# Neighbourhood attention: context and latent head pairs alternate, and GpSimd scales each pair's second head

## The chip, the cores and the metric

The kernel runs on one core of a Trainium2 chip. The metric is the device time of one execution, in microseconds (us). Before the change the median of three runs is 2026.64 us (2026.27 to 2027.99).

## What is computed

A two-layer backbone over 256 latent and 256 context tokens. The even layer's mixer has eight neighbourhood-attention heads of width 64 beside four mLSTM heads. The change touches the attention heads alone. Cut to what matters:

```python
def context_attention(q, k, v):                      # 256 context queries, 256 context keys
    s = jnp.einsum('bqhd,bkhd->bhqk', q, k) * (q.shape[-1] ** -0.5)
    p = jax.nn.softmax(s, axis=-1)
    return jnp.einsum('bhqk,bkhd->bqhd', p, v)

def neighbourhood_attention(q, k, v, k_ctx, v_ctx, rpb):   # 256 latent queries
    # one softmax over a clamped 4 x 16 window of the latent grid (with a learned bias)
    # and all 256 context keys
    logits = concatenate([s_loc + bias, s_ctx], -1)
    p = softmax(logits)
    return p_loc @ vwin + p_ctx @ v_ctx
```

The kernel computes the latent rows against all 512 tokens, context first, and a bias of -1e30 takes out the latent keys that are outside the window.

## The kernel before, in words

Each engine has its own program, written out by hand; semaphores tie them together. Attention is done in 32 units: a head pair `hp` (0 to 3), a stream `st` (0 context with 256 keys, 1 latent with 512 keys), a tile `qt` of 128 queries (0 or 1) and one of the pair's two heads `hh`. Two units that differ only in `hh` form a pair `p` of the loops (0 to 15). In this document "first head" and "second head" are these two, and a "round" is the four pairs of one `hp`.

What happens to pair `p`:

- TensorE `scores(p)` (L880) writes both heads' scores into two of four score banks.
- VectorE `maxima(p)` finds the negated row maximum. For a context unit that is one reduction from the bank (L2192). For a latent unit it is a copy of the context columns (L2194), an addition of the bias (L2195) and a reduction over 512 columns (L2196).
- ScalarE `exps(p)` (L1464) takes the exponential into `probs` and sums the rows.
- VectorE takes the reciprocal of the sums (L2204) and multiplies each head's probabilities by it (L2207).
- TensorE transposes them in 128x128 blocks (L909): 2 blocks for a context unit, 4 for a latent one.
- ScalarE `turned_probs(p)` (L1475) copies them to `probsT`.
- When both query tiles of a stream are there, TensorE `weigh` (L892) multiplies them with the values. VectorE `attention_out` (L2291) copies the result out.

The order in which VectorE works is `maxima(p + 1)`, then reciprocal and multiplications of pair `p`. TensorE does `scores(p + 2)`, then the transposes of `p`, then perhaps a `weigh`. `maxima(p)` waits until the transposes of `p - 2` are done (semaphore `na_pT_done`), as it reuses their `probs` buffers.

Before the change the order within a head pair is context, context, latent, latent. In the program listings below, `L` and `R` are regions of SBUF in which `probs` lies, and `bank` is one of the eight PSUM banks.

Of the kernel before, what the change touches and what calls it, by code (L numbers as in the profile page):

```python
# [20 lines left out]
ALU = mybir.AluOpType  # L21
# [6 lines left out]
CTX, LAT = 256, 256  # L28
T = CTX + LAT
# [72 lines left out]
def build(nc, i, out, stop=None):  # L102

    stack = contextlib.ExitStack()
    with stack:
        def sb(name, shape):
            return stack.enter_context(nc.sbuf_tensor(name, shape, F32))
# [3 lines left out]
        def sem(name):  # L111
            if name not in sems:
                sems[name] = stack.enter_context(nc.semaphore(name))
            return sems[name]
# [87 lines left out]
        col = sb("col", [P, 12])  # L202
# [64 lines left out]
        probs = [L[:, 0:T], L[:, T:2 * T], R[:, 12288:12288 + T], R[:, 5120:5120 + T]]  # L267
# [99 lines left out]
        ret_s = view(R, 9216, 4, TT, LAT)  # L367


        UNITS = [(hp, st, hh, qt) for hp in range(4) for st in range(2) for qt in range(2) for hh in range(2)]  # L370
        NA_PAIRS = len(UNITS) // 2


# [175 lines left out]
        def _(pe):  # L549
# [270 lines left out]
            def even():  # L820
# [46 lines left out]
                def scores(p):  # L867
# [7 lines left out]
                    for u in (2 * p, 2 * p + 1):  # L875
                        hp, st, hh, qt = UNITS[u]
                        r0 = NA_DIM * hh
# [5 lines left out]
                def weigh(group):  # L883

                    hp, st = group // 2, group % 2
                    tiles = 2 if st == 0 else 4
                    pe.wait_ge(sem("na_pT_ready"), 4 * group + 4)
                    if group >= 2:
                        pe.wait_ge(sem("even_y0"), group - 1)
                    for kt in range(tiles):  # L890
                        for hh in range(2):
                            last = nc.tensor.matmul(banks[4 + group % 2][NA_DIM * hh:NA_DIM * (hh + 1), 0:CTX],  # L892
                                                    na_v[:, kt, (2 * hp + hh) * NA_DIM:(2 * hp + hh + 1) * NA_DIM],
                                                    probsT(st, hh)[:, kt, :], start=(kt == 0), stop=(kt == tiles - 1))
                            if kt == tiles - 1:
                                last.then_inc(sem("na_out_done"), 1)
# [3 lines left out]
                for p in range(NA_PAIRS):  # L900
                    if p + 2 < NA_PAIRS:
                        scores(p + 2)
                    for u in (2 * p, 2 * p + 1):
                        tiles = 2 if UNITS[u][1] == 0 else 4
                        pe.wait_ge(sem("na_probs_ready"), u + 1)
                        if p:
                            pe.wait_ge(sem("na_pT_ready"), u - 1)
                        for kt in range(tiles):
                            last = nc.tensor.transpose(banks[2 + u % 2][:, kt * P:(kt + 1) * P], probs[u % 4][:, kt * P:(kt + 1) * P], ident[:, :])  # L909
                        last.then_inc(sem("na_pT_done"), 1)  # L910
                    if p and p % 2 == 0:
                        weigh(p // 2 - 1)
                weigh(NA_PAIRS // 2 - 1)


# [195 lines left out]
        def _(act):  # L1111
# [291 lines left out]
            def even():  # L1403
# [53 lines left out]
                def exps(p):  # L1457

                    for u in (2 * p, 2 * p + 1):
                        st = UNITS[u][1]  # L1460
                        keys = CTX if st == 0 else T
# [5 lines left out]
                def turned_probs(p):  # L1467

                    for u in (2 * p, 2 * p + 1):
                        hp, st, hh, qt = UNITS[u]  # L1470
                        tiles = 2 if st == 0 else 4
                        act.wait_ge(sem("na_pT_done"), u + 1)
                        if p >= 4 and qt == 0:
                            act.wait_ge(sem("na_out_done"), 2 * (p // 2) - 2)
                        nc.scalar.activation(probsT(st, hh)[:, :, qt * P:(qt + 1) * P],  # L1475
                                             banks[2 + hh][:, 0:tiles * P].rearrange("p (a n) -> p a n", n=P), ACT.Copy).then_inc(sem("na_pT_ready"), 1)

# [128 lines left out]
        def _(dve):  # L1606
# [4 lines left out]
            def link(ins):  # L1611

                chain[0] += 1
                ins.then_inc(sem("dve_chain"), 1)
                dve.wait_ge(sem("dve_chain"), chain[0])
# [509 lines left out]
            def even():  # L2125
# [7 lines left out]
                for hd in range(HEADS):  # L2133
# [5 lines left out]
                    for j in (0, 1, 3, 4):  # L2139
                        sh = j - CONV // 2  # L2140
                        a, b = max(0, -sh), CTX - max(0, sh)
# [57 lines left out]
                for p in range(NA_PAIRS):  # L2199
                    if p + 1 < NA_PAIRS:  # L2200
                        maxima(p + 1)
                    a = 2 * (p % 2)
                    dve.wait_ge(sem("na_exp_done"), 2 * p + 2)
                    link(nc.vector.reciprocal(col[:, 8 + a:10 + a], col[:, 4 + a:6 + a]))  # L2204
                    for u in (2 * p, 2 * p + 1):
                        keys = CTX if UNITS[u][1] == 0 else T
                        nc.vector.tensor_scalar(probs[u % 4][:, 0:keys], probs[u % 4][:, 0:keys], col[:, 8 + u % 4:9 + u % 4], None,  # L2207
                                                ALU.mult).then_inc(sem("na_probs_ready"), 1)
                    if p >= 3 and p % 2:
                        attention_out(p // 2 - 1)  # L2210
                attention_out(NA_PAIRS // 2 - 1)


                dve.wait_ge(sem("even_acol_ready"), 2)
# [71 lines left out]
            def attention_out(group):  # L2286

                hp, st = group // 2, group % 2
                a, b = STREAMS[st]
                dve.wait_ge(sem("na_out_done"), 2 * group + 2)  # L2290
                nc.vector.tensor_copy(y[:, hp, a:b], banks[4 + group % 2][:, 0:CTX]).then_inc(sem("even_y0"), 1)  # L2291
# [102 lines left out]
        def _(pool):  # L2394
            def sums(name, c0):

                w = slice(c0, T)
                for d in range(KT - 1):
                    if name == "ffn2":
                        cosines(d)  # L2400
                    pool.wait_ge(sem("r_ready"), before("r_ready", name) + d + 1)
                    if d == 0:
                        nc.gpsimd.tensor_copy(rsum[:, w], h[:, 0, w]).then_inc(sem("sums"), 1)  # L2403
                    else:
                        nc.gpsimd.tensor_tensor(rsum[:, w], rsum[:, w], h[:, d, w], ALU.add).then_inc(sem("sums"), 1)  # L2405
                    at = stages.index(name)
                    pool.wait_ge(sem("sq"), (KT - 1) * at + halves(name, streams(name)[0]) + d + 1)
                    if d == 0:
                        nc.gpsimd.tensor_copy(rsq[:, w], sq[:, 0, w]).then_inc(sem("sums"), 1)
                    else:  # L2410
                        nc.gpsimd.tensor_tensor(rsq[:, w], rsq[:, w], sq[:, d % 2, w], ALU.add).then_inc(sem("sums"), 1)
                    pool.wait_ge(sem("sums"), before("sums", name) + 2 * d + 2)
                if name == "ffn2":
                    cosines(KT - 1)
# [24 lines left out]
            def causal(buf, way, fill=0.0):  # L2439

                sign = 1 if way == 0 else -1
                return nc.gpsimd.affine_select(out=buf, in_=buf, pattern=[[sign, P]], compare_op=ALU.is_ge, fill=fill,
                                               base=0, channel_multiplier=-sign)

            def even():

                nc.gpsimd.memset(L[:, 0:2560], 0.0)
                nc.gpsimd.memset(R[:, 4096:6144], 0.0).then_inc(sem("s5_zero"), 1)
                pool.wait_ge(sem("even_conv_done"), HEADS)
                nc.gpsimd.memset(R[:, 12288:13312], 0.0).then_inc(sem("s5_zero"), 1)  # L2450
                for k in range(1, len(BATCHES) // 2):
                    pool.wait_ge(sem("s5_local_written"), 16 * k)
                    nc.gpsimd.memset(R[:, 12288:12800], 0.0).then_inc(sem("s5_zero"), 1)
                pool.wait_ge(sem("s5_local_written"), 16 * (len(BATCHES) // 2))
                for b in range(2):
                    pool.wait_ge(sem(f"s5_ops_written{b}"), 32 * (len(BATCHES) // 2))
                nc.gpsimd.memset(ml_v[:, :, :, HDIM:VCOLS], 1.0).then_inc(sem("ml_ready"), 1)
                nc.gpsimd.memset(outside, 0.0).then_inc(sem("s5_zero"), 1)
                pool.wait_ge(sem("s5_zero"), 2 + len(BATCHES) // 2)
                for way in range(2):  # L2460
                    causal(outside[:, way, :], way, -1e30).then_inc(sem("ml_ready"), 1)
                sums("even", 0)
                centre("even")
                gains(1, "even", 0)
# [192 lines left out]
```

## Time and profile before

| | us |
|---|---|
| median of three runs | 2026.64 |
| the profiled execution | 2024.13 |
| its span | 2022.4 |
| TensorE busy in the span | 1917.7 |
| VectorE busy | 1263.6 |
| ScalarE busy | 644.7 |
| GpSimd busy | 290.5 |

The attention stage lies between 629.7 us (first scores) and 699.0 us (last output copied) of the span. A page of the profile gives shares over the whole span; what a change in this stage is worth has to be read from the stage itself, for which the views take a window.

### The profile page before, as it was taken

To read this page: it belongs to the slowest core of one execution; us is meant where nothing else is said; L and a number is where in the kernel's file an instruction comes from. 1 tells how busy PE (TensorE), PEld (TensorE's weight loads), DVE (VectorE), ACT (ScalarE), POOL (GpSimd) and SP (SyncE) were. 2 spreads that over 40 slices of the span, in tenths; PEclk is the share of its full clock that TensorE was granted. 3 is DMA by queue.
4 is the path that set the end of the run, shared out by engine and by line. 5 is a ranking of instruction groups with operands and counts; after the bars stand their busy time and mean duration, and the time that the engine had idled before them with its cause. 6 is when DMAs were issued, how large, how long until landed. Compare 5 with 4: busy or idle time off the path is not lost.

```text
span 2022.4 us, 24268 instructions
## 1 busy us (share of the span) xinstructions
PE 1917.7 (95%) x9246; PEld 1523.2 (75%) x9246; DVE 1263.6 (62%) x2215; ACT 644.7 (32%) x1093; POOL 290.5 (14%) x318
## 2 busy tenths in 40 slices
PE   5999999999998789899999989999999899989997
PEld 5888878885553454788887878888778867879997
DVE  7677776742883572777778357774777535464454
ACT  2322242323343431422224233222423232334442
POOL 0000001150000002400000231000044535130003
PEclk7999999998998899899999999999999999989999
DMA  9354535313360001355444233544134544214542
GB/s 361 126 204 170 206 142 162 135 54 125 115 231 9 1 1 42 121 201 198 177 161 183 95 150 121 203 179 155 73 117 190 222 180 177 84 42 167 186 164 108
DMA packets 43959, 290.12 MB, mean 143 GB/s; under 512 B 13916, under 2 KB 19676, under 8 KB 27232
## 3 DMA queue, kind: packets, MB, share of 16 engines
q1 hardware_dynamic: 34336, 270.08, 35.6%
q10 hardware_dynamic: 9536, 18.88, 2.5%
q8 instruction: 55, 0.90, 0.2%
q14 instruction: 32, 0.26, 0.0%
HBM read 272.16 MB, written 16.78 MB: 143 GB/s over the span
## 4 chain that ended last, share of the span: by engine, by line
PE 84%; DVE 9%; ACT 3%; DMA 2%; issue 1%; POOL 1%; SPq 0%; ACTq 0%; POOLq 0%; DVEq 0%
PE bank L613 13%; PE bank L618 13%; PE bank L615 13%; PE bank L670 7%; PE bank L679 6%; PE bank L676 6%; PE bank L807 4%; PE bank L804 3%; PE bank L791 3%; PE bank L1001 2%; PE bank L744 2%; PE bank L734 1%; PE bank L998 1%; DVE L L1729 1%; PE bank L956 1%
## 5 line engine op out<-in xcount | busy, mean ns | idle before, releaser
L1729 DVE CUSTOM_DVE_ANT_0 L<-slot 128x1024 f32<-128x1024 f32 x272 | 337.7, 1241 | 72.1 <-DMA slot<-in_ada_dram 64.9
L1185 ACT ACTIVATE w_hi<-slot 128x1024 fp32r<-128x1024 f32 x176 | 186.2, 1060 | 571.4 <-PE bank L618 559.2
L1786 DVE TENSOR_TENSOR w_lo<-slot,w_hi 128x1024 fp32r<-128x1024 f32 x176 | 216.9, 1235 | 217.8 <-ACT w_hi L1185 212.0
L613 PE MATMUL bank<-m_hi,w_hi 128*128 128x512 f32 (+1 forms) x1344 | 296.6, 363 | 3.2 <-ACT w_hi L1185 3.2
L615 PE MATMUL bank<-m_lo,w_hi 128*128 128x512 f32 (+1 forms) x1344 | 296.1, 362 | 0.0
L618 PE MATMUL bank<-m_hi,w_lo 128*128 128x512 f32 (+1 forms) x1344 | 296.1, 362 | 0.0
L613 PEld LDWEIGHTS bank<-m_hi,w_hi 128*128 128x128 f32 x1344 | 232.3, 189 | 43.1 <-ACT w_hi L1185 4.0
L615 PEld LDWEIGHTS bank<-m_lo,w_hi 128*128 128x128 f32 x1344 | 232.6, 189 | 39.3
L618 PEld LDWEIGHTS bank<-m_hi,w_lo 128*128 128x128 f32 x1344 | 232.6, 189 | 39.3
L1945 DVE TENSOR_TENSOR down_lo<-slot,down_hi 128x1408 fp32r<-128x1408 f32 x64 | 108.6, 1709 | 128.5 <-ACT down_hi L1235 128.3
L676 PE MATMUL bank<-g_lo,down_hi 128*128 128x512 f32 (+1 forms) x770 | 156.5, 351 | 0.1
L676 PEld LDWEIGHTS bank<-g_lo,down_hi 128*128 128x128 f32 x770 | 128.1, 193 | 19.6 <-DVE g_lo L1951 0.8
L1235 ACT ACTIVATE down_hi<-slot 128x1408 fp32r<-128x1408 f32 x64 | 87.6, 1377 | 158.0 <-PE bank L679 119.7
L2403 POOL COPY L<-h 128x512 f32<-128x512 f32 (+1 forms) x6 | 3.6, 607 | 910.1 <-DVE h L1826 910.1
L670 PE MATMUL bank<-g_hi_mid,down_hi 128*128 128x512 f32 (+1 forms) x420 | 99.6, 367 | 1.8 <-ACT g_hi_mid L1245 1.5
L679 PE MATMUL bank<-g_hi_mid,down_lo 128*128 128x512 f32 (+1 forms) x420 | 88.7, 347 | 0.0
L670 PEld LDWEIGHTS bank<-g_hi_mid,down_hi 128*128 128x128 f32 x420 | 72.3, 195 | 20.2 <-ACT g_hi_mid L1245 9.9
L807 PE MATMUL bank<-m,slot 128*128 128x512 f32 x192 | 85.5, 602 | 0.0
L679 PEld LDWEIGHTS bank<-g_hi_mid,down_lo 128*128 128x128 f32 x420 | 69.5, 189 | 9.9
L2405 POOL TENSOR_TENSOR L<-L,h 128x512 f32<-128x512 f32 (+1 forms) x36 | 43.7, 1213 | 219.9 <-DVE h L1826 219.4
L807 PEld LDWEIGHTS bank<-m,slot 128*128 128x128 f32 x192 | 36.7, 194 | 43.9 <-issue 43.9
L2424 POOL TENSOR_TENSOR h<-h,L 128x256 f32<-128x256 f32 x80 | 63.4, 829 | 36.4 <-DVE L L1855 36.4
(348 smaller groups left out, 2616.8 us busy)
## 6 DMA issues: line engine op xcount, KB each, us to landing
slot<-in_gateup_dram SPq DMA_DIRECT2D x44, 2048.0 KB, 7.5
slot<-in_ada_dram SPq DMA_DIRECT2D x34, 2048.0 KB, 7.5
slot<-in_down_dram SPq DMA_DIRECT2D x32, 1408.0 KB, 5.9
slot<-in_ev_in_dram SPq DMA_DIRECT2D x4, 2048.0 KB, 9.7
slot<-in_od_in_dram SPq DMA_DIRECT2D x4, 2048.0 KB, 10.1
R<-s_ops SPq DMA_DIRECT2D x16, 512.0 KB, 6.8
s_tables<-slot ACTq DMA_DIRECT2D x8, 768.0 KB, 3.3
R<-s_tables SPq DMA_DIRECT2D x8, 768.0 KB, 7.4
```

Source lines behind the costliest of these rows:

```text
L613: nc.tensor.matmul(bank[j][:, c0:T], w_hi[:, off, c, :], m_hi[:, c, c0:T], start=(c == 0), stop=False)
L615: nc.tensor.matmul(bank[j][:, c0:T], w_hi[:, off, c, :], m_lo[:, c, c0:T], start=False, stop=False)
L618: last = nc.tensor.matmul(bank[j][:, c0:T], w_lo[b][:, 2 * j + off, c, :], m_hi[:, c, c0:T], start=False, stop=(c == KT - 1))
L670: nc.tensor.matmul(out_d, down_hi[:, half, f % HALF, :], g_hi(f)[:, a:b], start=(f == 0), stop=False)
L676: nc.tensor.matmul(out_d, down_hi[:, half, f % HALF, :], g_lo[:, f, a:b], start=False, stop=False)
L679: last = nc.tensor.matmul(out_d, down_lo[k - 3][:, half, f % HALF, :], g_hi(f)[:, a:b], start=False, stop=(f == FT - 1))
L807: last = nc.tensor.matmul(banks[n % 4][:, c0:T], wslot(k)[:, j, c, :], m[:, c, c0:T], start=(c == 0), stop=(c == KT - 1))
L1185: nc.scalar.activation(w_hi[:, off, :, :].rearrange("p a b -> p (a b)"), slots[b][:, (2 * (f % 2) + off) * D:(2 * (f % 2) + off + 1) * D], ...
L1235: nc.scalar.activation(down_hi[:, half, :, :].rearrange("p a b -> p (a b)"), slots[k][:, half * HALF * P:(half + 1) * HALF * P], ACT.Copy) ...
L1729: ins = nc.vector.tensor_tensor_reduce(out=junk, in0=slots[k][:, t * D:(t + 1) * D], in1=csilu[s_], scale=1.0, scalar=0.0, op0=ALU.mult, o ...
L1786: nc.vector.tensor_tensor(w_lo[b][:, t, :, :].rearrange("p a b -> p (a b)"), slots[b][:, t * D:(t + 1) * D], w_hi[:, off, :, :].bitcast(F3 ...
L1945: nc.vector.tensor_tensor(down_lo[d % 2][:, half, :, :].rearrange("p a b -> p (a b)"), slots[3 + d % 2][:, half * HALF * P:(half + 1) * HA ...
```

## The change

The order of the units becomes context, latent, context, latent within a head pair. The `weigh` of a stream moves to where its second query tile has been transposed: the context one behind the fourth pair of its head pair, the latent one behind the first pair of the next. `attention_out` moves accordingly, and so does the wait in `turned_probs`. The multiplication of each pair's second head moves from VectorE to GpSimd, which now waits for the reciprocals through a new semaphore `na_rec_ready`. TensorE waits for the first head on `na_probs_even` and for the second on `na_probs_odd`.

```diff
-        UNITS = [(hp, st, hh, qt) for hp in range(4) for st in range(2) for qt in range(2) for hh in range(2)]
+        UNITS = [(hp, st, hh, qt) for hp in range(4) for qt in range(2) for st in range(2) for hh in range(2)]
...
-                    pe.wait_ge(sem("na_pT_ready"), 4 * group + 4)
+                    pe.wait_ge(sem("na_pT_ready"), 2 * (4 * hp + 3 + st))
...
-                        pe.wait_ge(sem("na_probs_ready"), u + 1)
+                        pe.wait_ge(sem("na_probs_odd") if u % 2 else sem("na_probs_even"), p + 1)
...
-                    if p and p % 2 == 0:
-                        weigh(p // 2 - 1)
+                    if p % 4 == 3:
+                        weigh(p // 4 * 2)
+                    if p % 4 == 0 and p:
+                        weigh(p // 4 * 2 - 1)
...
-                            act.wait_ge(sem("na_out_done"), 2 * (p // 2) - 2)
+                            act.wait_ge(sem("na_out_done"), 2 * (2 * (hp - 1) + st) + 2)
...
-                    link(nc.vector.reciprocal(col[:, 8 + a:10 + a], col[:, 4 + a:6 + a]))
-                    for u in (2 * p, 2 * p + 1):
-                        keys = CTX if UNITS[u][1] == 0 else T
-                        nc.vector.tensor_scalar(probs[u % 4][:, 0:keys], probs[u % 4][:, 0:keys], col[:, 8 + u % 4:9 + u % 4], None,
-                                                ALU.mult).then_inc(sem("na_probs_ready"), 1)
-                    if p >= 3 and p % 2:
-                        attention_out(p // 2 - 1)
-                attention_out(NA_PAIRS // 2 - 1)
+                    nc.vector.reciprocal(col[:, 8 + a:10 + a], col[:, 4 + a:6 + a]).then_inc(sem("na_rec_ready"), 1)
+                    dve.wait_ge(sem("na_rec_ready"), p + 1)
+                    keys = CTX if UNITS[2 * p][1] == 0 else T
+                    nc.vector.tensor_scalar(probs[a][:, 0:keys], probs[a][:, 0:keys], col[:, 8 + a:9 + a], None, ALU.mult).then_inc(sem("na_probs_even"), 1)
+                    if p >= 4 and p % 4 < 2:
+                        attention_out(2 * (p // 4) - 2 + p % 4)
+                for group in range(NA_PAIRS // 2 - 2, NA_PAIRS // 2):
+                    attention_out(group)
...
+                for p in range(NA_PAIRS):
+                    u = 2 * p + 1
+                    keys = CTX if UNITS[u][1] == 0 else T
+                    pool.wait_ge(sem("na_rec_ready"), p + 1)
+                    nc.gpsimd.tensor_scalar(probs[u % 4][:, 0:keys], probs[u % 4][:, 0:keys], col[:, 8 + u % 4:9 + u % 4], None,
+                                            ALU.mult).then_inc(sem("na_probs_odd"), 1)
```

On TensorE (L880 scores, L909 transposes, L892 `weigh`, of which a latent one is eight rows and a context one the row with x4), before, from the transposes of a round's first latent pair on:

```order
L909 MATMUL bank<-ident,L 128x128 x8
L892 MATMUL bank<-L,R 64x256 x4
L880 MATMUL bank<-R 128x256 x2
L909 MATMUL bank<-ident,R 128x128 x8
L880 MATMUL bank<-R 128x512 x2
L909 MATMUL bank<-ident,L 128x128 x4
L892 MATMUL bank<-L,R 64x256
L892 MATMUL bank<-R 64x256
```

The same engine now, from the transposes of a round's last latent pair to those of the next round's first latent pair:

```order
L909 MATMUL bank<-ident,R 128x128 x8
L892 MATMUL bank<-L,R 64x256 x4
L880 MATMUL bank<-R 128x256 x2
L909 MATMUL bank<-ident,L 128x128 x4
L892 MATMUL bank<-L,R 64x256
L892 MATMUL bank<-R 64x256
...
L880 MATMUL bank<-R 128x512 x2
L909 MATMUL bank<-ident,R 128x128 x8
```

The context `weigh` has moved from in front of a latent pair's transposes to in front of a context pair's. The latent `weigh` has moved from behind a context pair with another context pair to follow, to behind a context pair with a latent pair's scores and transposes to follow.

On VectorE, before, from the reciprocal of a round's second context pair on (L2194 to L2196 are the maxima of a latent unit):

```order
L2204 RECIPROCAL col<-col 128x2 [waits na_exp_done]
L2207 TENSOR_SCALAR R<-R,col 128x256 [waits dve_chain]
L2207 TENSOR_SCALAR R<-R,col 128x256
L2291 COPY m<-bank5 128x256 [waits na_out_done]
L2194 COPY R<-bank7 128x256 [waits na_scores_done,na_pT_done]
```

VectorE now, at the same place of a round, with the line numbers of the changed file (the reciprocal is L2206, the multiplication L2209, the context reduction L2194):

```order
L2206 RECIPROCAL col<-col 128x2 [waits na_exp_done]
L2209 TENSOR_SCALAR L<-L,col 128x256 [waits na_rec_ready]
L2293 COPY m<-bank4 128x256 [waits na_out_done]
L2194 TENSOR_REDUCE col<-bank0 128x1 [waits na_scores_done,na_pT_done]
L2194 TENSOR_REDUCE col<-bank1 128x1 [waits na_scores_done]
L2206 RECIPROCAL col<-col 128x2 [waits na_exp_done]
L2209 TENSOR_SCALAR R<-R,col 128x512 [waits na_rec_ready]
```

One multiplication stands behind each reciprocal where there were two, and context reductions stand between the work of two latent pairs.

## Rows read from the trace of the kernel before

**Rows 1.** Windows: the attention stage (busy us per engine, TensorE clock share, DMA)
```profile
628.00:700.00 72.00, 53.50 (x274) 29.30 (x274) 44.62 (x120) 35.99 (x99) 0.00 (x0) 0.76 0.00 1
```
**Rows 2.** Timeline of VectorE: start, duration, instruction [idle before, releaser]
```profile
630.51 1.42 DVE L2192 TENSOR_REDUCE col<-bank 128x1 f32<-128x256 f32 x4 [24.46 <-PE bank L880]
...
649.22 0.76 DVE L2192 TENSOR_REDUCE col<-bank 128x1 f32<-128x256 f32 x2 [1.61 <-PE bank L909]
649.90 0.15 DVE L2204 RECIPROCAL col<-col 128x2 f32<-128x2 f32 x1
...
651.23 0.42 DVE L2194 COPY L<-bank 128x256 f32<-128x256 f32 x1 [0.53 <-PE bank L909]
...
655.35 0.42 DVE L2194 COPY R<-bank 128x256 f32<-128x256 f32 x1 [0.20 <-PE bank L909]
...
658.12 0.15 DVE L2204 RECIPROCAL col<-col 128x2 f32<-128x2 f32 x1
...
660.86 0.76 DVE L2192 TENSOR_REDUCE col<-bank 128x1 f32<-128x256 f32 x2 [1.67 <-PE bank L909]
661.53 0.15 DVE L2204 RECIPROCAL col<-col 128x2 f32<-128x2 f32 x1
...
665.50 0.76 DVE L2192 TENSOR_REDUCE col<-bank 128x1 f32<-128x256 f32 x2 [2.27 <-PE bank L909]
...
680.56 0.76 DVE L2192 TENSOR_REDUCE col<-bank 128x1 f32<-128x256 f32 x2 [1.19 <-PE bank L909]
...
698.61 0.42 DVE L2291 COPY m<-bank 128x256 f32<-128x256 f32 x1 [4.05 <-PE bank L892]
```
**Rows 3.** Windows of the stage, columns as in rows 1 (clock is third from last)
```profile
634.00:643.00 9.00, 5.44 (x18) 2.44 (x16) 6.65 (x17) 4.36 (x11) 0.00 (x0) 0.50 0.00 1
...
648.00:658.00 10.00, 7.21 (x46) 3.62 (x44) 7.84 (x21) 5.76 (x16) 0.00 (x0) 1.00 0.01 2
658.00:665.00 7.00, 6.15 (x26) 4.04 (x27) 3.29 (x10) 2.96 (x9) 0.00 (x0) 0.51 0.00 0
...
689.00:695.00 6.00, 4.81 (x21) 3.35 (x22) 2.87 (x8) 2.01 (x5) 0.00 (x0) 0.50 0.00 0
```
**Rows 4.** Timeline of TensorE in the stage
```profile
635.09 2.08 PE L880 MATMUL bank<-R 64*128 64x512 f32 x4
...
648.09 1.09 PE L909 MATMUL bank<-ident,R 128*128 128x128 f32 x8
649.12 1.13 PE L880 MATMUL bank<-R 64*128 64x512 f32 x4
...
651.12 0.43 PE L892 MATMUL bank<-L,R 128*64 128x256 f32 x1
...
652.69 0.38 PE L892 MATMUL bank<-R 128*64 128x256 f32 x1
...
654.61 0.70 PE L909 MATMUL bank<-ident,R 128*128 128x128 f32 x4 [0.48 <-DVE R L2207]
...
658.85 1.97 PE L909 MATMUL bank<-ident,L 128*128 128x128 f32 x8 [2.91 <-DVE L L2207]
660.75 1.98 PE L892 MATMUL bank<-L,R 128*64 128x256 f32 x8
```
**Rows 5.** Groups by line and form, 628 to 700 us: VectorE's multiplication
```profile
L2207 DVE TENSOR_SCALAR L<-L,col 128x512 f32<-128x512 f32 x8 | 3.5, 484 | 0.1
L2207 DVE TENSOR_SCALAR L<-L,col 128x256 f32<-128x256 f32 x8 | 2.5, 351 | 0.1
```
**Rows 6.** GpSimd's tensor-scalar at L2436 (x: min/median/max ns), two windows
```profile
L2436 POOL TENSOR_SCALAR h<-h,lng,lnb x2: 772/773/774, 841.0 to 841.7; 128x512 f32<-128x512 f32 x2
...
L2436 POOL TENSOR_SCALAR h<-h,lng,lnb x8: 554/560/1229, 2014.7 to 2019.5; 128x256 f32<-128x256 f32 x8
```
**Rows 7.** VectorE's tensor-scalar at L1861 over the whole span
```profile
L1861 DVE TENSOR_SCALAR L<-L x10: 293/294/815, 411.6 to 2009.2; 128x256 f32<-128x256 f32 x10
```
**Rows 8.** Timeline at 1585 us: GpSimd and VectorE together
```profile
1584.64 2.87 POOL L2424 TENSOR_TENSOR h<-h,L 128x256 f32<-128x256 f32 x4
...
1585.39 0.81 DVE L1861 TENSOR_SCALAR L<-L 128x256 f32<-128x256 f32 x1
```

## Prediction, made before the changed kernel ran

> **What bounds the stage now.** I read the windows first, then VectorE's timeline, then TensorE's. The windows show that nothing is full in the 72 us of the attention stage: TensorE 53.5 us busy, VectorE 44.6, ScalarE 36.0, GpSimd none [rows 1]. So the stage is a chain that passes from engine to engine, and the timeline shows which. VectorE computes the maxima of a pair. Then it takes reciprocal and multiplications of the pair before, and then it sits idle until TensorE has transposed exactly those: all idle times before L2192 and L2194 from 649 us on end on L909 [rows 2]. I call the time from a pair's reciprocal to VectorE's next maxima the pair's turn. It holds the reciprocal, the multiplication, TensorE's queue and the transposes. Freeing VectorE from work that lies beside the transposes gives nothing; the turn counts.
>
> A round (four pairs) is then four maxima and four turns. Maxima take 655.35 to 658.12 = 2.77 us for a latent pair and 660.86 to 661.53 = 0.67 for a context pair [rows 2], so 6.88 a round in either order. Turns before: context 649.90 to 651.23 = 1.33; first latent 658.12 to 660.86 = 2.74; second latent 661.53 to 665.50 = 3.97 [rows 2]. 6.88 + 2 x 1.33 + 2.74 + 3.97 = 16.25, and the round from 649.22 to 665.50 is 16.28. The next, to 680.56, is 15.06. The first took 18.7 (630.51 to 649.22), the last with its end 18.5 (680.56 to 698.61 + 0.42). Together 68.5 us.
>
> The second number behind these is TensorE's clock: it is granted at 0.50 (1.2 GHz) in 634 to 643, at 1.00 (2.4 GHz) in 648 to 658, 0.51 in 658 to 665, and 0.50 in 689 to 695 [rows 3]. The fall at 658 comes while TensorE idles for 2.91 us during a latent pair's maxima [rows 4]; the rise comes after several us of unbroken work. Eight transposes take 1.97 us at the low level and 1.09 at the high; a latent pair's scores 2.08 and 1.13; a context `weigh` (8 rows of the trace) 1.98 at the low one [rows 4]. The latent `weigh` runs from 651.12 to 652.69 + 0.38 = 1.95 at the high one [rows 4]; twice that, 3.9, is my estimate for the low one, and half of 1.98, 1.0, for a context one at the high.
>
> **The multiplication on GpSimd.** VectorE takes 484 ns for 512 columns and 351 for 256 [rows 5]. GpSimd's nearest operation, L2436, which multiplies and adds, takes 772 ns and 554 with nothing in its way [rows 6]. Its slow cases reach 1229 [rows 6]. The trace of before has no single multiplication on GpSimd, so I bound it below by VectorE's own 484 and 351 and above by 1229, and take 772 and 554, the same form with one operation more.
>
> When does it start? Both engines are released by the same reciprocal, and both want SBUF. L1861 on VectorE, the same kind of operation, takes 293 ns at its fastest and 815 at its slowest [rows 7], and the slow one of 0.81 us lies inside GpSimd's L2424 [rows 8]: it was held 0.52 us. So the two don't run together. VectorE needs no hand-over between engines, so I take it as first; GpSimd starts when it ends. The Trainium skill, "SBUF — State Buffer", section "Who interferes with whom", says that a VectorE operation in a two-port mode and a GpSimd one exclude each other for a whole instruction and that the one issued first wins; by that rule the time comes out as in this sum or as in the third rival below, and the trace's 0.81 us agrees that one is held.
>
> Context turn, at the high clock: reciprocal to multiplication 0.19, first head 0.35, hand-over 0.06 (658.85 less the end of a 484 ns multiplication begun 0.19 after 658.12 [rows 2, 4, 5]), second head 0.55, hand-over 0.06, its two transposes 0.43 (four take 0.70, 0.27 of it for two), 0.05 to VectorE: 1.69 against 1.33, so 0.36 lost. What covered the second multiplication before was the first head's transposes; a GpSimd multiplication is longer than that cover. Second latent turn: 0.19 + 0.48 + 0.06 + 0.77 + 0.06 + 0.60 (four transposes, a little over half of 1.09) + 0.05 = 2.21 at the high clock. At the low one TensorE's scores of the pair after next, 2.08 us from the context turn's end, make the transposes wait: 2.08 + 1.97 - 0.67 + 0.1 = 3.5.
>
> **The moved order.** First latent turn: TensorE is now behind. After the context transposes stand the latent `weigh`, then a latent pair's scores, then the transposes; VectorE's part beside them is 0.67 of maxima. High: 1.95 + 1.10 + 1.04 - 0.67 - 0.1 = 3.3 (start to start, as 648.09 to 649.12; the 0.1 is the hand-over at either end). Low: 3.9 + 2.08 + 1.97 - 0.77 = 7.2. Before, this `weigh` ran beside a latent pair's maxima (651.12, inside 651.23 to 654), where 2.77 us hid it. What lies there now is the context `weigh`, 1.0 to 2.0 us, which before stood in the second latent turn and made it 3.97 instead of 2.74. VectorE's output copies stay beside TensorE's work, and ScalarE, 36 us busy of 72, has the exponentials done before each reciprocal as before; I cost both at nothing. If that cover went, each copy would cost 0.42. No DMA and no queue of SyncE is in the moved part; GpSimd has nothing else to do until the layer's norm.
>
> A round at the high clock: 6.88 + 2 x 1.69 + 3.3 + 2.2 = 15.8. With the second half low (context turn 2.0, second latent 3.5, after 2.8 us of idle TensorE as at 658): 17.4. Before: 15.06 and 16.28, mean 15.67. With the last round, for three rounds: from +0.4 to +5; I take +2.5. The first round starts the same way; at the low clock its sum is equal to before within 0.5 us, and as TensorE works more evenly there it may come back to the high clock earlier, worth up to 2.5: I take -1. The end: before 3.2 us from the last transposes to the last copy; now a context `weigh` and a latent one follow, 1.0 + 1.95 + 0.5 = 3.4 high, up to 6.4 low: I take +1. Sum +2.5 us. That is 2026.6 on the profiled execution's 2024.13; on the median of the runs, which is 2.5 above that execution, 2029.1.
>
> A measurement of this kernel can tell about 0.2%, 4 us, from no change.
>
> **Rivals.**
>
> 1. Faster. GpSimd's multiplication runs beside VectorE's without being held: context turns 1.33, latent 1.9 (0.36 x 8 and 0.3 x 4 less), and the evener TensorE work keeps the clock high in most of the stage. Rounds of 14.8 against 15.67, a first round of 16 against 18.7: -2.8 - 2.7 = -5.5, 2021.1. For it: 0.50 of clock in a round's latent half is worth 2 us a round [rows 3]. Against it: the held L1861 [rows 7, 8], and idle gaps of 2.8 us that are still there.
>
> 2. Slower. The latent `weigh` falls into the low clock. Each time it does, the first latent turn grows from 3.3 to 7.2. It decides from two of the three: +8, with some given back by the rise during that same long work: 2036. For it: it now stands 3.5 us behind a TensorE gap. Against it: a context `weigh` and scores fill part of that gap.
>
> 3. GpSimd gets SBUF first, and VectorE's first head waits 0.55 or 0.77 for it. Then the first head's transposes, four of them 1.0 us at the low clock, no longer lie beside the second multiplication: about +0.2 a context turn and +0.5 a latent one more, 8 and 8 of them less what TensorE's queue hides, +3.5: 2032.6.
>
> **How the numbers follow.** My forecast 0.53, rival 1 0.20, rival 2 0.14, rival 3 0.13. The forecast's own range is 2026 to 2033. Within 0.2% is 2022.6 to 2030.7: 0.37 of the forecast, 0.05 of rival 1, 0.04 of rival 3, in all 0.46. Slower: 0.14 of the forecast, all of rival 2 and 0.07 of rival 3: 0.35. Faster: the rest of rival 1 and a little of the forecast, 0.19. The range for 8 in 10 is 2020 to 2037: below rival 1's centre and to just above rival 2's.
>
> **What would show it.** In the profile after: GpSimd's multiplications at about 0.55 and 0.77 us, or longer with the wait counted in, starting when VectorE's end; VectorE's idle before a latent pair's maxima ended by transposes of second heads, these by GpSimd; context turns of 1.7 and first latent turns of 3.3 or more, with `weigh` and scores before the transposes; the stage some 71 us long from 630.5. It would be wrong if context turns stayed at 1.3, if the granted clock were high all through, or if the stage were unchanged and the difference lay outside it.

## The result and the profile after

The changed kernel takes 2033.61 us (median of 7 runs, 2031.95 to 2034.90) against 2026.13 us before (7 runs, 2025.27 to 2027.99): 7.5 us slower, ratio 1.0036 with a 95% interval of 1.0027 to 1.0046. The time lies in the forecast range for 8 in 10, 2020 to 2037, and a little above the forecast's own 2026 to 2033. But the likeliest single time was 2029.1, and 0.46 was given to a change too small to be told, so the sign was left open and the size was three times too small. Of the runs used below, one of e3_twoop (2796.34 us) and one of the kernel before (10853.08 us) fell in a slow state; the ratios leave them out, the medians don't.

The profiled execution after took 2034.90 us, its span 2033.2. First the attention stage (window, columns as in [rows 1]):

```profile
628.00:706.00 78.00, 57.02 (x275) 28.58 (x273) 39.04 (x103) 37.44 (x99) 23.39 (x16) 0.78 0.00 1
```

VectorE's busy time fell from 44.6 us [rows 1] to 39.0, as the change meant it to. GpSimd, idle in this stage before, is busy for 23.4 us with 16 instructions, 1.46 us each. The mean clock is 0.78 against 0.76. So the mean clock of the stage isn't what made it slower than before. Groups by line and form, GpSimd in this window:

```profile
L2468 POOL TENSOR_SCALAR R<-R,col 128x512 f32<-128x512 f32 x8 | 14.8, 1844 | 11.2 <-DVE col L2206 11.2
L2468 POOL TENSOR_SCALAR L<-L,col 128x256 f32<-128x256 f32 x8 | 8.7, 1082 | 52.6 <-DVE col L2206 52.6
```

These two answer to [rows 5]: VectorE needs 484 and 351 ns for the same work. Three windows answer to [rows 3] (the clock is third from last):

```profile
651.00:664.00 13.00, 8.00 (x50) 3.93 (x48) 8.30 (x23) 7.27 (x19) 4.02 (x3) 1.00 0.00 0
665.00:674.00 9.00, 8.24 (x34) 4.11 (x34) 4.87 (x13) 4.61 (x12) 3.06 (x3) 0.50 0.01 2
...
682.00:688.00 6.00, 6.00 (x22) 2.81 (x24) 3.27 (x9) 3.07 (x8) 1.86 (x1) 0.51 0.00 0
```

VectorE's timeline after, with the lines that answer to [rows 2] (the reciprocal is L2206 now, the context maxima L2194, the latent ones begin with L2196):

```profile
631.83 0.76 DVE L2194 TENSOR_REDUCE col<-bank 128x1 f32<-128x256 f32 x2 [24.47 <-PE bank L880]
...
649.93 0.42 DVE L2196 COPY R<-bank 128x256 f32<-128x256 f32 x1 [2.64 <-PE bank L909]
...
655.25 0.15 DVE L2206 RECIPROCAL col<-col 128x2 f32<-128x2 f32 x1
...
658.53 0.42 DVE L2196 COPY R<-bank 128x256 f32<-128x256 f32 x1 [1.62 <-PE bank L909]
...
661.31 0.16 DVE L2206 RECIPROCAL col<-col 128x2 f32<-128x2 f32 x1
...
663.17 0.76 DVE L2194 TENSOR_REDUCE col<-bank 128x1 f32<-128x256 f32 x2 [1.32 <-PE bank L909]
663.85 0.15 DVE L2206 RECIPROCAL col<-col 128x2 f32<-128x2 f32 x1
...
667.16 0.42 DVE L2196 COPY R<-bank 128x256 f32<-128x256 f32 x1 [2.64 <-PE bank L909]
...
672.72 0.15 DVE L2206 RECIPROCAL col<-col 128x2 f32<-128x2 f32 x1
...
677.14 0.42 DVE L2196 COPY R<-bank 128x256 f32<-128x256 f32 x1 [1.62 <-PE bank L909]
...
706.12 0.42 DVE L2293 COPY m<-bank 128x256 f32<-128x256 f32 x1 [2.08 <-PE bank L892]
```

The context turn at 661.31 is 1.86 us (before 1.33). The first latent turns at 655.25 and 672.72 are 3.28 and 4.42. The second latent turn at 663.85 is 3.31. The stage takes 631.83 to 706.54 = 74.7 us against 68.5, so +6.2. The rest of the execution, 2034.9 - 74.7 = 1960.2, is 4.6 above that of before (1955.6); 1.3 of these lie ahead of the stage. In the other kernels profiled below the rest is 1956.2 to 1959.5, with no work changed there, so I take such differences as what varies from execution to execution. These two lie at the ends of what was seen, and why isn't shown.

The chain of waits in the second round names the new link (start, duration, what; "issue" is time in which nothing is waited for):

```profile
661.39 0.08 DVE col L2206
661.48 0.08 issue
661.56 1.09 POOL L L2468
662.65 0.04 issue
662.70 0.45 PE bank L909 x2
663.15 0.02 issue
663.17 0.76 DVE col L2194 x2
663.93 0.08 DVE col L2206
664.01 0.08 issue
664.09 1.86 POOL R L2468
665.96 0.04 issue
666.00 1.13 PE bank L909 x4
```

VectorE's reciprocal is still in the chain, with 0.08 us; its multiplication has left it, and GpSimd's has taken the place. That holds for every context turn, but not for every latent one. TensorE's rows tell which:

```profile
657.40 1.09 PE L909 MATMUL bank<-ident,R 128*128 128x128 f32 x8
...
664.58 1.12 PE L909 MATMUL bank<-ident,R 128*128 128x128 f32 x4 [0.34 <-DVE R L2209]
666.00 1.11 PE L909 MATMUL bank<-ident,R 128*128 128x128 f32 x4 [0.31 <-POOL R L2468]
...
683.93 2.05 PE L909 MATMUL bank<-ident,R 128*128 128x128 f32 x8
```

At 666.00 TensorE waits for GpSimd. At 657.40 (the first latent turn of 3.28 us) and at 683.93 (the second one of the third round, at the low clock) it transposes both heads without a gap, straight behind the scores: there its own queue is the limit, and GpSimd had ended by 657.34 and 684.81.

### The profile page after: what moved, and what is told of

Same layout as the page of the kernel before. It is cut to its first block, busy times and chain, and to the rows that moved or that the text cites. A ratio compares the mean times of both kernels' runs of the same rounds, so it can differ in the third digit from the quotient of the medians.

```text
span 2033.2 us, 24268 instructions
## 1 busy us (share of the span) xinstructions
PE 1927.0 (95%) x9246; PEld 1527.3 (75%) x9246; DVE 1258.4 (62%) x2199; ACT 645.7 (32%) x1093; POOL 313.4 (15%) x334
## 4 chain that ended last, share of the span: by engine, by line
PE 83%; DVE 9%; ACT 3%; DMA 3%; POOL 1%; issue 1%; SPq 0%; ACTq 0%; POOLq 0%; DVEq 0%
PE bank L613 13%; PE bank L618 13%; PE bank L615 13%; PE bank L670 6%; PE bank L679 6%; PE bank L676 6%; PE bank L807 4%; PE bank L804 3%; PE bank L791 3%; PE bank L1003 2%; PE bank L744 2%; PE bank L734 1%; PE bank L1000 1%; DMA slot<-in_down_dram 1%; PE bank L958 1%; DVE L L1731 1%
## 5 line engine op out<-in xcount | busy, mean ns | idle before, releaser
L807 PEld LDWEIGHTS bank<-m,slot 128*128 128x128 f32 x192 | 37.0, 195 | 44.7 <-issue 44.6
```

What stands on the lines that cost most here:

```text
L807: last = nc.tensor.matmul(banks[n % 4][:, c0:T], wslot(k)[:, j, c, :], m[:, c, c0:T], start=(c == 0), stop=(c == KT - 1))
```

## Experiments

Each kernel but one had 5 rounds beside the kernel before (e4_behind had 3); the ratio is to the runs of before that it shared, whose medians were 2026.1 to 2026.5. "Stage" is measured as above, in the profiled execution: first maxima to the end of the last output copy.

| kernel | median us | ratio to before, 95% interval | stage us | GpSimd 512 / 256 columns, ns |
|---|---|---|---|---|
| before | 2026.13 | | 68.5 | |
| changed | 2033.61 | 1.0036 (1.0027 to 1.0046) | 74.7 | 1844 / 1082 |
| e1_order | 2026.00 | 1.0001 (0.9992 to 1.0010) | 66.3 | |
| e2_pool | 2030.15 | 1.0018 (1.0009 to 1.0027) | 73.9 | 1858 and 1780 / 1082 |
| e3_twoop | 2025.96 | 0.9995 (0.9985 to 1.0004) | 67.2 | 989 / 642 |
| e4_behind | 2037.60 | 1.0056 (1.0041 to 1.0071) | 80.5 | 1562 / 956 |
| e5_weigh | 2019.48 | 0.9967 (0.9955 to 0.9980) | 58.0 | |
| e6_weigh_pool | 2023.13 | 0.9985 (0.9976 to 0.9994) | 61.7 | |
| e7_old_twoop | 2027.06 | 1.0012 (0.9995 to 1.0028) | 68.8 | |
| e8_busy | 2023.87 | 0.9991 (0.9982 to 1.0000) | 63.2 | |
| e9_weigh_busy | 2019.71 | 0.9964 (0.9950 to 0.9978) | 60.2 | |
| e10_old_weigh | 2019.01 | 0.9968 (0.9956 to 0.9980) | 59.7 | |

**Order or engine?** e1_order keeps the new order and takes GpSimd out again:

```diff
+                    nc.vector.tensor_scalar(probs[a + 1][:, 0:keys], probs[a + 1][:, 0:keys], col[:, 9 + a:10 + a], None, ALU.mult).then_inc(sem("na_probs_odd"), 1)
...
-                    nc.gpsimd.tensor_scalar(...).then_inc(sem("na_probs_odd"), 1)
```

> The changed kernel with its new order, but both heads' multiplications on VectorE. My theory (GpSimd's multiplication lengthens every turn, the order costs little by itself): context turns return from 1.9 to 2.1 us to about 1.35 (high clock) and 1.65 (low), the second latent turns from 3.3 to about 2.3 to 3.0, the first latent turns stay at 3.3 or more; about 5 to 6 us less than the changed kernel, 2027 to 2029. Rival (the loss is the latent weigh that now stands in front of a latent pair's transposes): within 2 us of the changed kernel's 2033.6.

2026.0: the whole loss is gone, a little more than I expected, and the rival falls. Context turns are 1.34, or 1.75 where TensorE is at the low clock. Of the 8.4 us between the two stages, seven context turns hold 3.9 and seven latent ones 2.4 (the last pair of each kind has no maxima behind it). The granted clock over most of the stage rose as well, from 0.76 in the changed kernel to:

```profile
632.00:690.00 58.00, 40.70 (x216) 21.43 (x212) 40.86 (x111) 32.58 (x89) 0.00 (x0) 0.85 0.00 1
```

So a part of what GpSimd costs here comes by way of the clock; how much, isn't shown. The runs of e1_order lie apart: 4 of 11 at 2022.2 to 2024.1, 5 at 2028.4 to 2029.3, two between. I didn't find out what sets them apart.

e2_pool keeps the old order and has GpSimd:

```diff
-                    for u in (2 * p, 2 * p + 1):
-                        ... nc.vector.tensor_scalar(probs[u % 4] ...).then_inc(sem("na_probs_ready"), 1)
+                    nc.vector.tensor_scalar(probs[a] ...).then_inc(sem("na_probs_even"), 1)
...
+                    pool.wait_ge(sem("na_rec_ready"), p + 1)
+                    nc.gpsimd.tensor_scalar(probs[u % 4] ..., None, ALU.mult).then_inc(sem("na_probs_odd"), 1)
```

> The kernel before with its order, but each pair's second head multiplied on GpSimd. My theory: context turns 1.9 instead of 1.33 (8 times), first latent turns about 3.3 instead of 2.74 (4 times), second latent ones hidden behind TensorE's queue: 4 to 7 us more than before, 2030 to 2033. Rival (order is what costs): within 2 us of before's 2026.1.

2030.15, at the edge of what was expected; the stage is 5.4 us longer. The context turns were 1.86 from the second round on, the first latent ones 3.31. So GpSimd is the cost in either order. Under the old order it costs 3.7 us in the medians (before had 2026.5 in the same rounds), under the new one 7.6. The clock in 632 to 690 is 0.76 with and without GpSimd under the old order, where under the new one it differs.

**Why 1.08 and 1.85 us?** The nearest row had promised 0.55 and 0.77 [rows 6]. Either GpSimd is held for the rest, or its instruction is slow. e4_behind keeps the two engines apart, e3_twoop changes the form alone:

```diff
                     pool.wait_ge(sem("na_rec_ready"), p + 1)
+                    pool.wait_ge(sem("na_probs_even"), p + 1)
```

> The changed kernel, with GpSimd waiting also for VectorE's multiplication of the pair's first head, so that the two never overlap. If the 1.08 and 1.85 us hold a wait for VectorE, they shrink to about 0.75 and 1.4, end at the same time as before, and the kernel stays at 2033 to 2034. If GpSimd needs that long by itself, the durations stay, its ends come 0.3 and 0.45 us later, and the kernel is 3 to 5 us slower, 2037 to 2039.

```diff
-                    nc.gpsimd.tensor_scalar(..., col[:, 8 + u % 4:9 + u % 4], None, ALU.mult)
+                    nc.gpsimd.tensor_scalar(..., col[:, 8 + u % 4:9 + u % 4], 0.0, ALU.mult, ALU.add)
```

> The changed kernel, with GpSimd's instruction in the form multiply then add 0.0, the form of L2436, instead of a single multiply. If the single-operation form is slow by itself, the 1.08 and 1.85 us fall to about 0.85 and 1.2 (0.55 and 0.77 plus the time held by VectorE), and the kernel gets about 4 us faster, 2029 to 2030. If being held by VectorE or the operands make it slow, the durations stay within 0.1 us and the kernel stays at 2033 to 2034.

e4_behind gave 2037.6, as slow as the second theory said. But its durations are between the two. GpSimd's timeline in it, where it starts when VectorE has ended, and in the changed kernel, where it starts 0.06 us after VectorE's multiplication:

```profile
657.11 1.56 POOL L2469 TENSOR_SCALAR R<-R,col 128x512 f32<-128x512 f32 x1 [2.04 <-DVE R L2209]
```

```profile
664.09 1.85 POOL L2468 TENSOR_SCALAR R<-R,col 128x512 f32<-128x512 f32 x1 [1.45 <-DVE col L2206]
```

So being held makes up 1.85 - 1.56 = 0.29 us; the other 1.56 are its own. How much of them is the form, e3_twoop tells. Groups of GpSimd in e3_twoop, where nothing else was changed:

```profile
L2468 POOL TENSOR_SCALAR R<-R,col 128x512 f32<-128x512 f32 x8 | 7.9, 989 | 10.8 <-DVE col L2206 10.8
L2468 POOL TENSOR_SCALAR L<-L,col 128x256 f32<-128x256 f32 x8 | 5.1, 642 | 56.8 <-DVE col L2206 56.8
```

The instruction that also adds zero takes 0.99 us where the bare multiply takes 1.85, and the kernel is back at 2025.96. I had expected 2029 to 2030. The difference is in the latent turns: the second one of the second round fell from 3.31 to 1.99 (662.46 to 664.45), where I had counted on 0.6 less. GpSimd's part of that is 1.85 - 0.99 = 0.86 us. The rest is the clock: in the changed kernel it was granted at 0.50 in 664 to 667, where these transposes lie, and in e3_twoop at 1.00 in 660 to 664.

e7_old_twoop closes the square, the old order with the two-operation form:

```diff
-                        ... col[:, 8 + u % 4:9 + u % 4], None, ALU.mult ...
+                        ... col[:, 8 + u % 4:9 + u % 4], 0.0, ALU.mult, ALU.add ...
```

> The kernel before with its order, second head on GpSimd in the multiply-and-add-0.0 form. Completes the square of order and GpSimd form. If the form alone made the loss: context turns about 1.42 instead of 1.86 in e2_pool, latent 2.8 instead of 3.3; 2026 to 2028 against e2_pool's 2030.2. Rival (the form matters only beside the new order): 2030.

2027.06, with context turns of 1.42: as expected. One of its eleven runs took 2043.81 us and widens the interval; the others are 2024.9 to 2028.7. With the quick form GpSimd costs nothing that can be told from zero in either order, and it gains nothing either, though VectorE has less to do.

**What does the turn hold else?** If the turn is what counts, taking a `weigh` out of TensorE's queue in front of the transposes must pay, whichever engine multiplies. e5_weigh starts from e1_order:

```diff
                 for p in range(NA_PAIRS):
+                    if p % 4 == 2 and p > 4:
+                        weigh(p // 4 * 2 - 1)
                     if p + 2 < NA_PAIRS:
                         scores(p + 2)
...
-                    if p % 4 == 0 and p:
-                        weigh(p // 4 * 2 - 1)
...
-                    if p >= 4 and p % 4 < 2:
-                        attention_out(2 * (p // 4) - 2 + p % 4)
+                    if p >= 4 and p % 2 == 0:
+                        attention_out(2 * (p // 4) - 2 + p % 4 // 2)
```

> The new order with both multiplications on VectorE (as e1_order), and the latent weigh moved once more: from behind the next round's first context pair to in front of that round's second context scores, where TensorE idles beside a latent pair's maxima; its output copy moves along. My theory (a turn costs what stands in TensorE's queue in front of the transposes, and work in the idle gap also holds the clock high): the first latent turns fall from 3.3 to about 2.0 three times, and the turns behind the gaps run at the high clock; 4 to 8 us less than e1_order, 2018 to 2022. Rival (the latent weigh is hidden by something else anyway, or ScalarE's copies, which now wait for it, hold up the exponentials): within 2 us of e1_order's 2026.

2019.48, 6.5 us less than e1_order. VectorE's timeline of a round of it:

```profile
651.15 0.15 DVE L2206 RECIPROCAL col<-col 128x2 f32<-128x2 f32 x1
...
653.01 0.42 DVE L2196 COPY R<-bank 128x256 f32<-128x256 f32 x1 [0.79 <-PE bank L911]
...
655.78 0.16 DVE L2206 RECIPROCAL col<-col 128x2 f32<-128x2 f32 x1
...
657.12 0.76 DVE L2194 TENSOR_REDUCE col<-bank 128x1 f32<-128x256 f32 x2 [0.20 <-PE bank L911]
657.80 0.15 DVE L2206 RECIPROCAL col<-col 128x2 f32<-128x2 f32 x1
...
659.71 0.42 DVE L2196 COPY R<-bank 128x256 f32<-128x256 f32 x1 [0.84 <-PE bank L911]
```

The first latent turn is 1.86 us, the context turn 1.34, the second latent one 1.91. The round from 653.01 to 666.36 takes 13.35 us, where before had 16.28 and 15.06. The window over most of the stage shows that the clock stayed up too (e1_order, from which this kernel starts, had 0.85). Before:

```profile
632.00:690.00 58.00, 42.80 (x208) 22.35 (x208) 40.87 (x110) 31.40 (x87) 0.00 (x0) 0.76 0.00 1
```

e5_weigh:

```profile
632.00:690.00 58.00, 40.19 (x252) 21.58 (x250) 43.71 (x119) 33.72 (x96) 0.00 (x0) 0.94 0.00 1
```

e6_weigh_pool makes the same moves on top of e3_twoop:

```diff
+                    if p % 4 == 2 and p > 4:
+                        weigh(p // 4 * 2 - 1)
```

> The same move of the latent weigh, with the second head on GpSimd in the multiply-and-add-0.0 form (as e3_twoop). My theory: as e5_weigh, less 0.3 a context turn and 0.4 a latent one that GpSimd's 0.64 and 0.99 us cost over VectorE: 2 to 4 us slower than e5_weigh, 2021 to 2025. Rival (VectorE's freed time pays): faster than e5_weigh.

2023.13, 3.7 us slower than e5_weigh, as expected: context turns of 1.42 and latent ones of 1.99 against 1.34 and 1.86, and a later end. Where the rest of the turn is short, GpSimd's 0.64 and 0.99 us show again, although VectorE is less busy.

**How much is the clock?** e8_busy adds matmuls of no use to e1_order and changes nothing else:

```diff
+                    if p % 4 == 2:
+                        for _ in range(5):
+                            nc.tensor.matmul(banks[4][:, CTX:T], ident[:, :], na_v[:, 0, 0:CTX], start=True, stop=True)
```

> e1_order with five 128x128 by 256 matmuls of no use in each round, put where TensorE idles for 2.8 us beside the second latent pair's maxima (about 2.1 us at the high clock), writing to an unused half of a bank. They can only cost, unless the granted clock matters. If low-clock turns are what a busier TensorE would win back: the clock of the stage rises from 0.85 towards 1.0, 2 to 5 us less than e1_order, 2021 to 2024, and its two groups of runs (2022 to 2024 and 2028 to 2029) become one. Rival: no change or slower, 2026 to 2028, as the added work delays the transposes.

2023.87, 2.1 us less than e1_order, and the mean clock in 632 to 690 rose from 0.85 to 0.94. The direction fits, but the runs of the two kernels overlap (2020.5 to 2026.4 here), so I call it supported rather than shown. Of e5_weigh's 6.5 us some 2 may then be the clock and the rest the shorter queue; that split is an estimate.

**Does the gain need the new order?** e10_old_weigh is the kernel before with the context `weigh` of the same round put into the idle stretch:

```diff
+                    if p % 4 == 2:
+                        weigh(p // 2 - 1)
                     for u in (2 * p, 2 * p + 1):
...
-                    if p and p % 2 == 0:
+                    if p and p % 4 == 0:
                         weigh(p // 2 - 1)
```

> The kernel before, its order and both multiplications on VectorE, with one move: the context weigh goes from behind the transposes of a round's first latent pair to in front of them, where TensorE idles for 2.9 us beside the second latent pair's maxima. Tests whether the gain of e5_weigh needs the new order. My theory (it does not): second latent turns fall from 3.3 to 4.0 to about 1.9 to 2.0, and with the gap filled the first latent turns run at the high clock, 1.9 instead of 2.7; 2.3 to 2.9 us a round, 8 to 10 us in all, bounded by e5_weigh: 2017 to 2021. Rival (the alternation is needed as it spreads TensorE's work): 2023 to 2026.

2019.01, 7.1 us faster than before by one moved `weigh`. The second latent turn, 3.97 us in before at 661.53, is 1.87 (660.02 to 661.89). The first latent turn, in whose queue nothing was moved, fell too, from 2.74 to 1.86: its transposes ran at the high clock now. The alternation isn't needed. e9_weigh_busy fills the last gaps of e5_weigh with useless work:

```diff
+                    for _ in range(5 if p in (0, 2) else 2 if p % 4 == 0 else 0):
+                        nc.tensor.matmul(banks[5][:, CTX:T], ident[:, :], na_v[:, 0, 0:CTX], start=True, stop=True)
```

> e5_weigh with useless 128x128 by 256 matmuls where TensorE still idles beside a latent pair's maxima: five each in the two gaps of the first round, two in the first gap of each later round. In e5_weigh the stage is at 0.95 of the full clock and only the first round is partly low, so there is little left: 0 to 2 us less than e5_weigh, 2017.5 to 2019.5, and a narrower spread than its 2015 to 2022. Rival (the spread of e5_weigh comes from outside the stage): the spread stays.

2019.71 from 5 runs, 2015.8 to 2020.2: no gain; the spread is 4.4 us against 6.7, from one run fewer. The profiled stage is even longer than e5_weigh's, 60.2 us against 58.0. The turns are the same; what differs is the stretch from the last latent pair's maxima to the last copy: from the reciprocal before it, 681.48 to 691.28 = 9.8 us here and 682.49 to 689.27 = 6.8 in e5_weigh. The granted clock was 0.56 in 684 to 691 here and 1.00 in 684 to 690 there. So one thing that varies is the clock at the stage's end; whether it makes the spread of the runs isn't shown. e5_weigh, e9_weigh_busy and e10_old_weigh all beat both kernels and can't be told from each other.

## Why the prediction was right in part

The frame held. The stage is a sum of maxima and turns. Measured in the three parts the forecast used, with their sum (each after against before):

| part | forecast | measured |
|---|---|---|
| first round (to the maxima behind its last transposes) | -1 | 649.93 - 631.83 = 18.1 against 18.7: -0.6 |
| three rounds, to the last transposes | +2.5 | 649.93 to 701.64 = 51.7 against 649.22 to 695.90 = 46.7: +5.0 |
| the end | +1 | 4.9 against 3.1: +1.8 |
| sum | +2.5 | +6.2 |

- *The multiplication on GpSimd: too small, and the step that failed.* I took 772 and 554 ns, "the same form with one operation more", and bounded it above by 1229. It is 1844 and 1082. Counted from the reciprocal to the end of GpSimd's work, with the wait for VectorE in both, that is 1.33 us against 1.15 for a context pair and 2.09 against 1.50 for a latent one. e4_behind and e3_twoop split the 1844: 0.29 us held by VectorE, and 0.86 between the bare multiply and multiply-and-add (1.85 against 0.99, both held). That one operation more costs time was an assumption, and here the form with one operation less is the slow one. e3_twoop shows that this is the term that mattered: with the quick form alone the kernel is back at 2025.96. The trace of before had the hint in rows that I left aside: its only single-operation case on GpSimd, a maximum at 1725 us, took 1.49 and 1.77 us for 512 columns. I put it down to VectorE beside it.
- *The context turn:* 1.69 forecast, 1.86 measured at the high clock, 2.12 at the low (2.0 forecast). *The second latent turn:* 2.2 forecast at the high, 3.5 at the low. All three measured are 3.31, for two reasons. In the first and third rounds the clock was low and TensorE's own queue made it, as the 3.5 had it. In the second round (663.85) the clock was high up to the scores, but TensorE waited for GpSimd, and the transposes then ran at the low clock, 1.11 us for four. With the measured turns the second round is 6.88 + 1.86 + 3.28 + 1.86 + 3.31 = 17.19 (17.23 measured) and the third 6.88 + 2.12 + 4.42 + 2.12 + 3.31 = 18.85 (18.85).
- *The moved order:* the first latent turn, 3.3 forecast, was 3.28, 4.42 and 3.29, and 3.29 in e1_order without GpSimd, so TensorE's queue makes it, as forecast. The 4.42 had the latent `weigh` partly at the low clock, 3.0 us instead of 1.9. So rival 2's mechanism was there once and for a third of its price. The order alone costs about nothing in sum, as e1_order showed (1.0001): its first latent turns are longer (3.29 against 2.74) and its three second ones in sum shorter (8.5 us against 10.1).
- *Who is held:* VectorE went first each time, at its full speed (0.49 and 0.35 us); rival 3, near in number with 2032.6, didn't happen. The Trainium skill, "SBUF — State Buffer", section "Who interferes with whom", has the later one blocked until the first has ended; here it starts in the record 0.06 us behind and gets 0.29 us longer, where VectorE's multiplication had 0.43 us left. A part of GpSimd's fixed time may lie in the wait; no run here tells.
- *Rival 1* is out with the form as it was; e3_twoop reached 2025.96, still not faster than before. Removing VectorE work that lay beside transposes gained nothing, as said.
- *The chances:* slower had 0.35. With the measured durations in the forecast's own sum, eight context turns get 0.17 us longer (1.86 against 1.69) and up to four latent ones 0.6: 1.4 to 3.8 us, an estimate of 2030.5 to 2032.9, where 2033.61 was measured. Slower would have been the likelier case. What is left lies in the low clock of the third round (4.42) and of the end, which the forecast had named but not put in its centre.

## What to carry to other kernels

Before moving an operation to another engine, look for that operation in that very form on that engine, and distrust a bound from a neighbouring form: adding a useless second operation nearly halved the time here. In a chain that passes from engine to engine, count what stands in each queue in front of the awaited instruction. An idle engine's gap is the place for work that nobody waits for soon: moving one `weigh` a round into such a gap was worth 7 us, through a shorter queue and a clock that stays up, and freeing some 6 us of VectorE nothing.

## What the runs showed of the hardware

- GpSimd's tensor-scalar over f32, 128 partitions, one scalar per partition: a single multiply 1.56 us for 512 columns and 0.92 to 0.93 for 256 with VectorE not beside it; multiply then add 0.0 takes 0.99 and 0.64 while held at its start.
- TensorE's mean granted clock in 632 to 690 us was 0.88 (e10_old_weigh) and 0.94 (e5_weigh, e8_busy) where gaps of about 2.8 us beside latent maxima held a `weigh` or useless matmuls, against 0.76 before and 0.85 in e1_order. In before it fell from 1.00 to 0.51 at 658 us, in a gap of 2.91 us.
